# Modulation vectors of a second block and of its experts: from matmuls in the scan stage to VectorE sums in the attention stage

## The reference

```python
# first block
mod = silu(c) @ w_ada + b_ada                  # 1024 x 3072: shift, scale, gate
h = rms_norm(x, g) * (1 + scale) + shift
proj = h @ w_in
y_r = rwkv7_mix(...)        # a chunked linear recurrence, 8 heads of 64, gated by silu(g_r)
y_a = chunk_band_attention(...)                # 8 heads of 64, gated by silu(g_a)
x = x + gate * (concat(y_r, y_a) @ w_out)
# second block
mod = silu(c_2) @ ada_w_2 + ada_b_2            # 1024 x 6144: sh_m, sc_m, g_m, sh_f, sc_f, g_f
h = rms_norm(x) * (1 + sc_m) + sh_m
x = x + g_m * (hybrid_mixer(h) @ w_out_2)
h = rms_norm(x) * (1 + sc_f) + sh_f
x = x + g_f * hierarchical_moe(h)              # 32 experts, top 2
out = rms_norm(x)
```

## Time and profile before

| | us |
|---|---|
| median of 3 runs | 1447.54 (1445.89 to 1452.07) |
| the profiled execution's own time | 1450.88 |
| its span, first to last instruction | 1449.1 |
| PE busy | 1297.0 (89%) |
| DVE busy | 567.5 (39%) |
| ACT busy | 346.1 (24%) |
| POOL busy | 158.1 (11%) |
| mean granted TensorE clock | 0.959 |

### The profile page before, as it was taken

How to read it: one execution, slowest core, us unless ns; L and a number is a source line. 1 busy time by engine, 2 the same in 40 slices (tenths; PEclk the granted TensorE clock), 3 DMA queues, 4 the chain that set the end, 5 groups by cost and what they waited for, 6 DMA issues and landing times.

```text
span 1449.1 us, 21053 instructions
## 1 busy us (share of the span) xinstructions
PE 1297.0 (89%) x7518; PEld 644.0 (44%) x7519; DVE 567.5 (39%) x1074; ACT 346.1 (24%) x751; POOL 158.1 (11%) x276
## 2 busy tenths in 40 slices
PE   5989999999899999999999795799899878898786
PEld 2445656568854444644454344333333322333222
DVE  1356372745123333358786635212212211222124
ACT  1223232323134442212454421011101100101012
POOL 4011110201020000000000001211021111111110
PEclk9999999999999999999999896799999999999999
DMA  9250806142073110032110384189999999999994
...
DMA packets 40047, 303.86 MB, mean 210 GB/s; under 512 B 7852, under 2 KB 8004, under 8 KB 22560
## 3 DMA queue, kind: packets, MB, share of 16 engines
...
...
## 4 chain that ended last, share of the span: by engine, by line
PE 68%; DMA 20%; DVE 5%; issue 3%; POOL 2%; ACT 2%; SPq 0%; DVEq 0%; ACTq 0%; POOLq 0%
PE bank L828 21%; DMA arena<-in_w_down 14%; PE bank L2769 9%; PE bank L759 8%; PE bank L2785 6%; PE bank L874 4%; DMA arena<-in_w_gu 3%; PE bank L837 2%; PE bank L817 2%; DMA arena<-in_ada_w 2%; PE bank L2759 1%; PE bank L1134 1%; DMA arena<-bias_scratch 1%; PE bank L1056 1%; PE bank L1072 1%
## 5 line engine op out<-in xcount | busy, mean ns | idle before, releaser
L828 PE MATMUL bank<-hT,arena 128*128 128x512 f32 x768 | 342.9, 602 | 0.0
L2769 PE MATMUL bank<-arena,hT 128*64 128x512 f32 x1024 | 231.6, 600 | 29.1 <-DMA arena<-in_w_gu 27.5
L828 PEld LDWEIGHTS bank<-hT,arena 128*128 128x128 f32 x768 | 145.0, 192 | 175.2 <-issue 172.0
L2769 PEld LDWEIGHTS bank<-arena,hT 128*64 128x64 f32 x1024 | 71.3, 137 | 167.7 <-issue 136.1
L2785 PE MATMUL bank<-arena,yT 128*64 128x512 f32 x512 | 125.9, 637 | 15.8 <-DMA arena<-in_w_down 15.8
L759 PE MATMUL bank<-arena,yT 128*128 128x512 f32 x256 | 115.6, 606 | 2.3 <-DVE yT L1629 2.3
L2929 DVE TENSOR_SCALAR hT<-hT 128x256 f32<-128x256 f32 x32 | 9.4, 294 | 250.9 <-ACT hT L2880 250.9
L759 PEld LDWEIGHTS bank<-arena,yT 128*128 128x128 f32 x256 | 48.7, 195 | 61.4 <-issue 57.1
L2785 PEld LDWEIGHTS bank<-arena,yT 128*64 128x64 f32 x512 | 36.0, 145 | 81.8 <-issue 62.7
L874 PEld LDWEIGHTS bank<-arena 64*64 64x64 f32 x1856 | 59.3, 135 | 27.9 <-issue 14.4
L2880 ACT ACTIVATE hT<-bank 128x256 f32<-128x256 f32 x32 | 12.3, 383 | 248.7 <-PE bank L2769 248.7
...
## 6 DMA issues: line engine op xcount, KB each, us to landing
...
```

Source lines behind the costliest of these rows:

```text
L828: last = T.matmul(bank[0:rows, :], w[:, k, 0:rows], hT[:, k, :], start=k == 0, stop=k == KD - 1)
L2769: last = T.matmul(banks[1 + ub][MT * h:MT * h + MT, :], tile.xT[:, k, :], wgu[u][:, k // 4, :, k % 4, 256 * h:256 * h + 256], start=k == 0 ...
```

## The change

- The host hands over `ada_w_2` transposed: 48 blocks of 128 x 1024 (0.5 MB each, 8 for each vector), so that output `n` of a vector lies in a partition and the 1024 weights behind it lie along the row. `silu(c_2)` is written to DRAM once and read back into all partitions (`spread_c`, the first 1024 columns of the tile `side`).
- DVE makes each block's 128 sums by one `tensor_tensor_reduce` over 128x1024, in place in one of four slots: 4 before `center`, 4 before `pair_out`, 4 before the wait for the attention bias, and 36 spread over 15 attention steps (`MOD_STEPS`). SP loads the blocks behind certain projection weights (`mod_after`), and each load past the fourth waits for the sum four before it.
- PE's `ada_step` is gone from the pairs. The gate projection, formerly whole in level 4, is cut into eight single matmuls (`gate_step`) at level 4, level 5, and six later places of the pair. The first two matmuls of projection 1 stand before level 1. ACT's and DVE's parts of the gate (`proj_raw(q, 3)`, `proj_shift(q, 3)`) move to the end of the pair.
- Bank 7 becomes free for the planner. Two stores of gates stand at the end of POOL's first part and wait for the last sums.

```diff
                     plan(("gram", p, h, j), "dve")
             if p:
                 plan(("mean", p - 1), "dve")
+            else:
+                free_banks[0].append(ADA_BANK)
+            if q:
+                plan_held(("proj", q, 1))
             for l in range(1, LEVELS):
                 plan(("W", p, l), "act")
-                if l <= 4 and q:
+                if l <= 3 and q:
                     plan_proj(q, PROJ_ORDER[l - 1])
+                if l == LEVELS - 3 and q:
+                    plan_held(("proj", q, 3))
                 if l <= 2 and not q:
                     plan(("va", l - 1), "act")
                 if l < LEVELS - 1:
...
                 plan(("U", p, c), "act")
                 if c + 1 < TT:
                     plan(("S", p, c), "dve")
+            if q:
+                plan_proj(q, 3)
             plan(("Y", p), "act")
         plan(("va", 2), "act")
         plan(("mean", PAIRS - 1), "dve")
...
                                  A[w].rearrange("(p k) n -> p k n", k=KD)[:, k, at * 512:(at + m) * 512]
                                  ).then_inc(ada_sem[ada_slot(n)[0]], 16)
                     ada_sent[0] += 1
+
+            mod_sent = [0]
+
+            def load_mod(count):
+
+                for n in range(mod_sent[0], mod_sent[0] + count):
+                    if n >= MOD_SLOTS:
+                        sp.wait_ge(s_ada_used, PE_ADA + n - MOD_SLOTS + 1)
+                    else:
+                        sp.wait_ge(filled, fill_at[("Y", PAIRS - 1)] + 1)
+                    sp.dma_start(mod_w[n % MOD_SLOTS], A["ada_w_2"][n // KD, n % KD]).then_inc(ada_sem[n % MOD_SLOTS], 16)
+                mod_sent[0] += count
...
+                load_mod(mod_after.get(name, 0))
                 if name == ("aproj", 1, 1):
                     sp.wait_ge(s_pair, PAIRS)
-                    sp.wait_ge(s_modst, 16 * 4)
+                    sp.wait_ge(s_modst, 16)
...
             load_w_out(1, w_out2_v)
             assert ada_sent[0] == len(ada_loads)
 
-        ada_after = {("proj", 0, 3): KD + 1, ("proj", 1, 3): KD, ("proj", 2, 3): KD, ("proj", 3, 3): KD - 1}
+        ada_after = {("proj", 0, 3): KD}
+        mod_after = {("aproj", 0, 2): 4, ("aproj", 1, 0): 4, ("aproj", 1, 1): 4, ("aproj", 2, 0): 4, ("aproj", 2, 1): 1,
+                     ("aproj", 2, 2): 3, ("aproj", 3, 0): 5, ("aproj", 3, 1): 3, ("aproj", 3, 2): 3, ("glu_a", 0): 5,
+                     ("glu_b", 0): 3, ("glu_a", 1): 3, ("glu_b", 1): 6}
+        assert sum(mod_after.values()) == MOD_BLOCKS
 
 
         def pool_block1(eng):
...
+                w, at, m = ada_groups[1]
+                eng.wait_ge(s_mod, 2)
+                eng.dma_start(mod_dram[at * 512:(at + m) * 512].rearrange("(c n) -> c n", n=512),
                               mod_row[0:32 * m:32, :]).then_inc(s_modst, 16)
-                if g + 1 < 5:
-                    eng.wait_ge(s_modst, 16 * g)
-                    bias_load(g + 1)
-
-            def mod_cols(i, at):
-                eng.dma_start(modc[i], mod_dram[at:at + DM].rearrange("(p k) -> p k", k=KD)).then_inc(s_modld, 16)
+
+            def spread_c():
+
+                eng.wait_ge(s_cact, 1)
+                eng.dma_start(c_dram.rearrange("(p k) -> p k", k=KD), cact[:, KD:2 * KD]).then_inc(s_modst, 16)
+                eng.wait_ge(s_modst, 32)
+                eng.dma_start(side[:, 0:DM], bass.AP(c_dram.tensor, 0, [[0, P], [1, DM]])).then_inc(s_modld, 16)
+                eng.dma_start(side[:, DM:DM + MOD_BLOCKS], A["ada_b_2"]).then_inc(s_modld, 16)
 
             bias_load(1)
 
...
                     done(G.tensor_copy(er[0:8, 575:ERL], er[0:8, 574:575].to_broadcast([8, ERL - 575])))
 
                     eng.dma_start(er_dram, er[0:8, 0:ERL].unsqueeze(1).to_broadcast([8, COPIES, ERL])).then_inc(s_biasst, 16)
-            eng.wait_ge(s_modst, 16 * 4)
-            mod_cols(2, 3 * DM)
-            mod_cols(3, 4 * DM)
-            mod_cols(4, 6 * DM)
-            mod_cols(5, 7 * DM)
             eng.wait_ge(s_pair, PAIRS)
             eng.wait_ge(s_biasst, 16)
...
+            for i, at in ((4, 5 * DM), (5, 8 * DM)):
+                eng.wait_ge(s_mod, 3)
+                eng.dma_start(mod_dram[at:at + DM].rearrange("(p k) -> p k", k=KD),
+                              mod2[:, i * KD:(i + 1) * KD]).then_inc(s_modst, 16)
 
 
...
             full(last)
+
+        def proj_part(name, bank, ks):
+
+            w = chunk_ready(name)
+            for k in ks:
+                last = T.matmul(bank[:, :], w[:, k, :], hT[:, k, :], start=k == 0, stop=k == KD - 1)
+            if KD - 1 in ks:
+                full(last)
 
         def pe_rows(name, src):
 
...
             for p in range(PAIRS):
                 q = p + 1 if p + 1 < PAIRS else None
-                ada_k = [0]
-
-                def ada_step():
+                gate_k = [0]
+
+                def gate_step():
                     if q:
-                        pe_ada(2 + p, ada_k[0])
-                        ada_k[0] += 1
+                        name, k = ("proj", q, 3), gate_k[0]
+                        gate_k[0] += 1
+                        proj_part(name, begin(name) if k < KD - 1 else fill(name), (k,))
 
                 eng.wait_ge(s_ops, 3 * p + 1)
                 for c in range(TT):
@@ -942,7 +985,10 @@
                 gram_up(p, 2, 1, t_b)
                 if p:
                     mean(p - 1)
-                ada_step()
+                else:
+                    eng.wait_ge(s_mod, 2)
+                if q:
+                    proj_part(("proj", q, 1), begin(("proj", q, 1)), (0, 1))
                 for l in range(1, LEVELS - 1):
                     eng.wait_ge(s_lf, (LEVELS - 2) * p + l)
                     if l == 1:
...
                     blocks(("W", p, l), Lfc[l % 2], Dc, (0, 1))
-                    if l <= 4 and q:
+                    if l == 1 and q:
+                        proj_part(("proj", q, 1), fill(("proj", q, 1)), range(2, KD))
+                    elif l <= 3 and q:
                         pe_proj(("proj", q, PROJ_ORDER[l - 1]))
                     elif l <= 2:
                         pe_rows(("va", l - 1), hT)
-                    elif l == LEVELS - 2:
-                        ada_step()
+                    elif l in (LEVELS - 3, LEVELS - 2):
+                        gate_step()
                     wait_emptied(eng, ("W", p, l))
                     if l > 1:
...
-                ada_step()
+                        out_chunk(c, fill(("Y", p), 2 * (TT - 1 - c) - (0 if q else 1)))
+                gate_step()
                 wait_emptied(eng, ("U", p, TT - 1))
                 full(out_chunk(TT - 1, fill(("Y", p))))
-                assert ada_k[0] == (KD if q else 0)
+                assert gate_k[0] == (KD if q else 0)
             pe_rows(("va", 2), hT)
             mean(PAIRS - 1)
             pe_rows(("va", 3), hT)
             variance(PAIRS - 1)
...
                     if l == 2 and q:
                         key_square(q)
-                    if l <= 4 and q:
+                    if l <= 3 and q:
                         proj_raw(q, l - 1)
...
                     empty(S, "act", S.activation(Ut[:, c, :], bank[:, 0:P], ACT.Copy), ("U", p, c))
                 if q:
+                    proj_raw(q, 3)
...
 
         def dve_ada(g):
-            w, at, m, _ = ada_groups[g]
+            w, at, m = ada_groups[g]
             V.wait_ge(s_adaw, 16 * (g + 1))
-            if g > 1:
-                V.wait_ge(s_modst, 16 * (g - 1))
             V.wait_ge(s_ada_used, KD * (g + 1))
             dve.done(V.tensor_tensor(mod_row[0:32 * m, :], banks[ADA_BANK][0:32 * m, :], ada_bias[0:32 * m, :], ADD))
             V.sem_inc(s_mod, 1)
+
+        mod_done = [0]
+
+        def mod_blocks(count):
+
+            for n in range(mod_done[0], mod_done[0] + count):
+                V.wait_ge(ada_sem[n % MOD_SLOTS], 16 * ((PE_ADA + n) // MOD_SLOTS + 1))
+                w = mod_w[n % MOD_SLOTS]
+                V.tensor_tensor_reduce(out=w, in0=w, in1=side[:, 0:DM], scale=1.0, scalar=0.0, op0=MUL, op1=ADD,
+                                       accum_out=mod2[:, n:n + 1]).then_inc(s_ada_used, 1)
+            mod_done[0] += count
+
+        def mod_biased(first, last):
+
+            assert last * KD <= mod_done[0]
+            V.wait_ge(s_ada_used, PE_ADA + last * KD)
+            at = slice(first * KD, last * KD)
+            dve.done(V.tensor_tensor(mod2[:, at], mod2[:, at], side[:, DM:DM + MOD_BLOCKS][:, at], ADD))
+
+        MOD_FIRST = 12
+        MOD_STEPS = [1, 3, 3, 2, 3, 3, 3, 2, 3, 3, 3, 2, 2, 2, 1, 0]
+        assert MOD_FIRST + sum(MOD_STEPS) == MOD_BLOCKS and MOD_FIRST + sum(MOD_STEPS[:12]) >= 4 * KD
 
         def dve_block1(eng):
...
                     proj_shift(q, 2)
                     operands(q)
                 level_add(p, 4)
-                if q:
-                    proj_shift(q, 3)
                 l = LEVELS - 2
                 bank = take(V, ("D", p, l))
...
```

(16 more changed lines are left out.)

67 lines of the change are left out of this document (32 added, 35 removed).

## The result

The change makes the kernel slower, by somewhat less than 1%: 1461.22 us against 1452.07 us (medians of 7 runs each). The two medians divide to 1.0063; the record's own ratio, with its 95% interval, is 1.0088 (1.0067 to 1.0108). Both lie above 1. The forecast was 1444.8 with a range from 1434 to 1455. The profiled execution has a span of 1462.1 us, 13.0 more than before.

The account below looks back on a forecast made before the run. The prediction took PE to bound both scan and attention, with DVE and DMA looking free in attention. Pairs -18.2, entry +11.6 and attention +3.9 summed to -2.7 us; less 3.3 for the profiled execution's excess, 1444.8, range 1434 to 1455.

Parts of the forecast that it names:

- rival (d): Pairs, level 4 gives nothing net: slow stretches and thin cover leave -10.4 us there, 1452.6 in all; chance 0.11.
- D runs from about 215.3 ... the rest becomes a PE wait of some 3.5 us: Level 4: of 6.2 us taken from the chain 2.7 are won; PE waits some 3.5 for DVE.
- Lower bound 13.4, if the new wait in level 4 brings a slow stretch each time, which costs 1.6 us: Pairs: least gain 13.4 us, if PE's clock drops behind each new level 4 wait, 1.6 us each.
- Blocks ahead of center and pair_out, 8.8 us: Way into attention: two rounds of loading and summing four blocks make `pair_out` end 8.8 us late.
- The bias takes 1.2 longer: Way into attention: SP's weights, in flight from the start, slow the bias's first 0.48 MB, 1.2 us more.
- The 23.3 that the prediction set beside it: Bias load: by turns of 2 KB against 4 KB, a third of 270 GB/s, 23.3 us; whole change +2.0.
- The first scores wait for the bias: Entry: the bias is the last thing awaited; it lands 10.0 us later, so scores start at 440.0, not 430.0.
- Three blocks last until 458.9, so the fourth step comes 0.85 later, three times: Attention: sums in a pair's third step delay the fourth step's scores by 0.85 us; three times, 2.6 us.
- DVE has no one waiting for it in that step: Attention: blocks behind `w_out` may land up to 20 us after issue, costing nothing until PE's projection is done.
- Fifteenth step 1.3: Attention: one block lies ahead of the row block PE already waits 2.3 us for, costing 1.3 us.
- (b): Entry covered by PE's 21 us of projections: only the late variance counts, -10.9 us, 1436.6; chance 0.29.
- (c): DVE sums slow, 2.2 us a block instead of 1.25: +8.7 us, 1456.2; chance 0.12.

Follow-up runs that it names:

- pairs only: Changed kernel without modulation weight loads and sums (vectors are the bias alone, not the reference's): 1420.0 us, so only its stages are read.
- all sums after pair_out: Changed kernel with the first twelve sums behind `pair_out`, still ahead of the wait for the bias: 1452.7 us, one run.
- sums without loads: Changed kernel with the 48 sums run on data already there, 25 MB not loaded: 1425.4 us, one run; only its stages are read.
- loads without sums: Changed kernel with each block loaded and waited for, one column copied in place of the sum: 1428.3 us, one run; only stages read.
- the last two of the table: Changed kernel with loads and sums reordered: gate matmuls 2, 1, 1, 1, 1, 1, 0, 1 took 1440.9 us; gate as made 1435.3 us.
- gate whole: Changed kernel with all eight gate matmuls in level 4 again, their ACT and DVE parts at the old places: 1465.8 us, ratio to before 1.0078.
- gate 4 and w_out late: Changed kernel with four gate matmuls in level 4, w_out in four pieces behind later projection weights, w_fvd behind the last: 1448.7 us.
- all of these: Changed kernel with four gate matmuls in level 4, first blocks asked for earlier, w_out late, sums and loads reordered: 1430.7 us, ratio to before 0.9845.

## Why the prediction was wrong

The mechanisms were mostly the right ones. Three terms were mis-sized, all by leaving out what comes with a wait: the slow stretch behind it, or the waits of the engine that hands work over. A fourth part, 4.5 us, is the place of before (see the result). In the pairs rival (d) came nearest, -10.4 for -10.9, but by luck: it had 4.8 us of slow stretches and 3 of thin cover, and measured are 12.2 of the first, against more work saved.

**Pairs: -18.2 forecast, -10.9 measured.** *"D runs from about 215.3 ... the rest becomes a PE wait of some 3.5 us"*: right, 3.3. *"Lower bound 13.4, if the new wait in level 4 brings a slow stretch each time, which costs 1.6 us"*: the step that failed. The stretch came in each pair and cost 12.2 us in all. I had priced it by a stretch in attention, 3.6 us long, and chose the case without any. Over the seven kernels that have waits of 2.4 to 2.9 us in level 4, the granted clock of the window behind the wait is under 1.00 in 19 of 21 pairs (after, pairs only, all sums after pair_out, sums without loads, loads without sums, and the last two of the table); in the five with four gate matmuls there and a longest wait of 0.8 to 1.1 it is 1.00 in 15 of 15. A long wait isn't the only road to it: "gate whole" has none over 1.0 us for ACT and lost more. Without the stretches the pairs would have won 10.9 + 12.2 = 23.1, more than the upper bound of 20. 0.8 of this was won ahead of the first transposes and 1.7 is the slow stretch of before's first pair, so the work taken off PE is some 20 us, where the forecast had 18.2. Whether the gate's matmuls between the chunk links can be left out at no cost was not tried alone.

**Entry: +10.0 forecast, +14.6 measured.** *Blocks ahead of center and pair_out, 8.8 us*: 10.0. The first of the four blocks could be summed 7.1 us after its issue, where the forecast has some 4.9 (the weight's 3.4 and one block's 1.45); the others came 1.27 apart instead of 1.45. The late start isn't a rule: with gate 4 and w_out late the same loads were there 5.3 us after their issue, and `pair_out` at +28.2. *The bias takes 1.2 longer*: 409.49 to 428.39 is 18.9 us, 1.5 more than the 17.4 of the earlier trace rows. The 23.3 that the prediction set beside it didn't come, but not because queues don't take turns. It had taken one row for one packet, 2 KB against 4 KB. The trace's packets, from 415 to 428, where both queues have work:

```profile
DMA packets 977, 3.41 MB, mean 262 GB/s; under 512 B 145, under 2 KB 145, under 8 KB 977
q1 hardware_dynamic: 487, 1.79, 53.3%
q0 software_dynamic: 490, 1.61, 49.8%
```

Here q0 is POOL's queue with the bias, q1 SP's with the weights. Without the 145 tiny ones a packet is 3.41 MB / 832 = 4.1 KB in the mean, and none reaches 8 KB; so a packet of the bias holds two of its rows. The two queues moved 490 and 487 packets. With packets of one size, turns give the bias a half, not a third. This trace agrees with the rule of the Trainium skill (DMA: Bandwidth & Descriptors, section on queues, rings and completion order) that each DMA engine takes packets from its queues in turn. *The first scores wait for the bias*: wrong, and named among the things that would make the forecast fail. I followed the third group only as traffic beside the bias, and not as four DMAs that DVE waits for, in program order, ahead of the bias. That is 3.2 us; with all sums behind pair_out it is 8.1 (scores 10.2 behind the bias, before 2.1).

**Attention: +5.5 forecast, +9.1 measured.** *Three blocks last until 458.9, so the fourth step comes 0.85 later, three times*: the two later ones measure 0.53 and 0.78 more, right in size. *DVE has no one waiting for it in that step* (a late block behind w_out): wrong. Block 12 came 9.44 us late in the first step, DVE carried it to the fourth step, and that wait is 2.36 longer; with w_out later, 0.53. *Fifteenth step 1.3*: 1.2. In the thirteenth step a wait of 1.62 is new, which the forecast doesn't have. It isn't the sums' doing. All fourteen traces sort by the clock just ahead of it: the five with 1.00 there have the wait (two of them without sums in that step), the nine with 0.66 or less don't. At the low clock PE takes longer over the work ahead (before: 1.55 us for L1072, 0.88 after) and comes when DVE's rows are ready.

**Rivals.** (b), the entry is covered, failed as the kernel stood, and is what "all of these" makes true. (c), slow sums, failed: 1.22 to 1.23 us each, beside any traffic. The range ended at 1455 since each rival moved one term; three terms moved together. A slowdown by more than 0.5%, which is what came, had a chance of 0.15. The mistake they share: a new wait was priced by its own length at the place where it stood, for PE without the clock behind it, for DVE without what stands behind it in its program.

One thing looks like scatter and is mostly not. Between kernels with the same code up to there the pairs end at 371 to 379 with one-tile steps, and at 361 to 370 with four in level 4. Take off the start of the first pair (85.3 to 88.9) and half the length of each stretch at the low clock. Then the six kernels with the gate as made need 279 to 280 us for the pairs, the one with two in level 4 276.9, the five with four there 274 to 275.5, "gate whole" 275.7, and before 299.4. So the split itself is worth some 5 us, the change saved some 20, and the rest is the clock: stretches of 3.4 to 17.1 us, of which the record doesn't say why they are long or short. With four in level 4 they stand in the last pair, which has no gate work, in some runs and not in others; from 345 to 360 first the kernel with four in level 4 alone, then all of these:

```profile
345.00:360.00 15.00, 13.28 (x126) 11.38 (x124) 2.28 (x5) 2.62 (x6) 0.00 (x0) 1.00 0.01 2
```

```profile
345.00:360.00 15.00, 13.67 (x83) 12.12 (x85) 1.68 (x4) 2.27 (x5) 0.00 (x0) 0.57 0.00 1
```

The windows show that it fell, not why. No run here covers that pair.
